# Output projections of two attention layers begun on the finished heads, during the last head's attention

## The chip, the core and the metric

The kernel runs on one core of a Trainium2 chip. Its engines work beside each other, each through its own list of instructions in order: TensorE (PE), VectorE (DVE), ScalarE (ACT), GpSimd (POOL) and SyncE (SP, which issues loads). They meet at semaphores. The metric is the device time of one execution in microseconds, the median of the runs; less is better.

## The reference

A network of six mixing and two feed-forward layers in float32, for 512 tokens of width 1024. The change touches the ends of the first two layers. Both have the same form: heads of attention, each times a gate, side by side as `y` (512 x 1024), then `y @ w_out`, a norm and the residual sum.

```python
# layer 0, dilated: 16 heads of 64, three groups of keys per head, joined by their log-denominators
y = o.reshape(B, S, DIL_WIDTH).astype(h.dtype) * jax.nn.silu(gate)
return y @ w_out
# layer 1, differential: 8 heads of 128
a = p[:, 0] - lam * p[:, 1]
o = rmsnorm(o, subln) * (1.0 - lambda_init)
y = o.reshape(B, S, DIFF_WIDTH) * jax.nn.silu(gate)
return y @ w_out
# around each layer
h = h + rmsnorm(y, norm_post[i])
```

## The kernel before

**Products.** Each float32 matrix is split in two parts of a narrower type: the high part (`uh`, `wh`) is a copy by ACT, the low part (`ul`, `wl`) the difference, which DVE makes for the input and POOL for the weights. A product is three matmuls (`three`, L418): high with high, low with high, high with low.

**Weights.** They stream in tiles of 128 x 1024. SP loads a tile into one of two slots of `raw` (L328) in two halves, once POOL has done the half that was there; ACT writes `wh` (`split`, L979), once the tile four back is used up (`tile_used`); POOL writes `wl` (L389) and signals `lo_ready`. From the first output projection on, `wh` and `wl` are rings of four slots.

**The dilated layer** works in stages of ten input tiles. A stage projects one pair of heads and computes the attention of the pair before it, a piece behind each tile: scores (L485), maxima on DVE (L1624), exponentials on ACT (L1099), weights on DVE (L1727), transposes on PE (L581), copies to `H` on ACT (L1146), and behind the last block PV (L593 to L606) and the gated result into `F` on DVE (L1714). `dil_last` computes the last pair, 7, with no tile beside it. "Head 7" below means this pair, and k counts the pairs: k is also the row block of `w_out` that goes with it. **The differential layer** has four tiles in a stage and the same scheme (transposes L492, values L497); its output is normed on DVE (L1776 to L1788), turned by PE (L678) and gated (L1796). The last stage is `diff_stage(None, 7, 0)`.

**Barriers.** `bound()` drains PE, ACT and DVE and lets none go on before the three have come to it. One stands ahead of each of the two projections.

**The output projection** has its tokens in the rows: 4 token blocks (t) by 2 column halves of 512, 8 k of 128 each. The first column half uses tiles b to b+3 (`tok_block`): tile j for the four blocks, two k each, banks 0 to 3. The second half uses b+4 to b+7 (`last_tokens`), block 0 with all four tiles first, then block 1, then 2 and 3 by turns, banks 4 to 7, beside the norms of the blocks that are done. ACT copies F to `uh` (`split_input`, L1031), DVE makes `ul` (`split_lo`, L1584): k = 0 and 1 ahead of the barrier, k = 2 to 7 behind it. PSUM has eight banks; scores use 2 and 3 (the dilated last head also 0 and 1), transposes 4 and 5, outputs 6, V's transposes 7. The next layer's first tiles start by token halves (`first_tiles`) in the banks that the projection used first.

The order of the work is the order in which each engine's function is written. ACT also issues DMAs: the gains (`ask_gain`) and, behind PV of the last dilated head, the input x into `H`, which held the weights until then (L1190).

## Time and profile before

| | |
|---|---|
| median of 3 runs | 2588.49 us (2584.99 to 2589.3) |
| profiled execution | 2583.04 us, span 2581.2 us |
| PE busy | 2409.3 us, 93% |
| DVE, ACT, POOL busy | 1184.4, 1102.8, 1036.0 us |
| mean granted clock of TensorE | 0.968 of full |

Times within the execution count from the start of the span. The profile's rows give the start, the busy time, the line and what is written and read; the number in square brackets is how long the engine idled before it, and who ended that.

### The profile page before, as it was taken

To read this page: it belongs to the slowest core of one execution; us is meant where nothing else is said; L and a number is where in the kernel's file an instruction comes from. 1 tells how busy PE (TensorE), PEld (TensorE's weight loads), DVE (VectorE), ACT (ScalarE), POOL (GpSimd) and SP (SyncE) were. 2 spreads that over 40 slices of the span, in tenths; PEclk is the share of its full clock that TensorE was granted. 3 is DMA by queue.
4 is the path that set the end of the run, shared out by engine and by line. 5 is a ranking of instruction groups with operands and counts; after the bars stand their busy time and mean duration, and the time that the engine had idled before them with its cause. 6 is when DMAs were issued, how large, how long until landed. Compare 5 with 4: busy or idle time off the path is not lost.

```text
span 2581.2 us, 40224 instructions
## 1 busy us (share of the span) xinstructions
PE 2409.3 (93%) x13062; PEld 1959.2 (76%) x13062; DVE 1184.4 (46%) x2431; ACT 1102.8 (43%) x2396; POOL 1036.0 (40%) x750
## 2 busy tenths in 40 slices
PE   7999999997999969997999999999888999999998
PEld 6777777776877748775878888888755878888887
DVE  4455554552667754266443432222776324522224
ACT  4433333334544435454554533232565544533322
POOL 4444343433433303451471354444411652444442
PEclk9999999997999969998999999999998999999999
DMA  5333333323322212220341233232212331232322
GB/s 189 103 96 94 93 99 91 94 82 103 94 82 79 74 35 74 83 89 25 101 145 50 82 107 98 91 100 94 88 52 66 115 123 50 94 98 94 98 89 82
DMA packets 126067, 232.02 MB, mean 90 GB/s; under 512 B 17120, under 2 KB 17248, under 8 KB 125920
## 3 DMA queue, kind: packets, MB, share of 16 engines
q1 hardware_dynamic: 123072, 219.56, 27.5%
q10 hardware_dynamic: 2848, 10.49, 1.1%
q8 instruction: 95, 1.56, 0.3%
q14 instruction: 52, 0.43, 0.1%
HBM read 208.48 MB, written 2.10 MB: 82 GB/s over the span
## 4 chain that ended last, share of the span: by engine, by line
PE 45%; issue 29%; POOL 10%; DVE 6%; DVEq 4%; ACT 3%; ACTq 1%; DMA 1%; POOLq 0%; SPq 0%
PE PS L418 39%; POOL wl L389 10%; DVEq L1500 3%; PE PS L485 2%; DVE work L1661 1%; PE PS L497 1%; DVE work L1657 1%; ACTq L1100 1%; DVE work L1624 1%; ACT work L1099 1%; DVEq L1625 1%; PE PS L606 1%; PE PS L630 1%; PE PS L581 0%; DVE work L1727 0%
## 5 line engine op out<-in xcount | busy, mean ns | idle before, releaser
L389 POOL TENSOR_TENSOR wl<-raw,wh 128x512 fp32r<-128x512 f32 x746 | 1035.7, 1411 | 1517.6 <-ACT wh L979 1516.3
L418 PE MATMUL PS<-uh,wh 128*128 128x512 f32 (+1 forms) x2120 | 801.0, 378 | 21.8 <-DVE ul L1550 8.5
L418 PE MATMUL PS<-uh,wl 128*128 128x512 f32 (+1 forms) x2120 | 785.9, 371 | 0.0
L418 PE MATMUL PS<-ul,wh 128*128 128x512 f32 (+1 forms) x2120 | 784.6, 370 | 0.0
L979 ACT ACTIVATE wh<-raw 128x512 fp32r<-128x512 f32 x746 | 430.1, 623 | 373.5 <-PE PS L418 319.5
L418 PEld LDWEIGHTS PS<-uh,wh 128*128 128x128 f32 x2120 | 404.9, 191 | 104.7 <-issue 17.7
L418 PEld LDWEIGHTS PS<-uh,wl 128*128 128x128 f32 x2120 | 403.6, 190 | 68.3
L418 PEld LDWEIGHTS PS<-ul,wh 128*128 128x128 f32 x2120 | 404.7, 191 | 64.0 <-issue 1.0
L418 PE MATMUL PS<-wh,hid_sb 128*128 128x512 f32 x1024 | 322.1, 396 | 0.0
L1118 ACT ACTIVATE work<-PS 128x512 f32<-128x512 f32 (+1 forms) x156 | 89.8, 575 | 404.6 <-PE PS L418 331.8
L418 PEld LDWEIGHTS PS<-wh,hid_sb 128*128 128x128 f32 x1024 | 192.4, 188 | 46.1
L418 PE MATMUL PS<-wl,hid_sb 128*128 128x512 f32 x512 | 202.5, 395 | 0.0
L418 PE MATMUL PS<-wh,uh 128*128 128x512 f32 x448 | 177.6, 396 | 8.6 <-DVEq L1495 6.5
L418 PE MATMUL PS<-wh,ul 128*128 128x512 f32 x448 | 176.5, 394 | 0.0
L418 PE MATMUL PS<-wl,uh 128*128 128x512 f32 x448 | 176.3, 394 | 0.0
L485 PE MATMUL PS<-work 64*32 64x128 f32 (+8 forms) x1568 | 144.8, 363 | 20.5 <-DVEq L1949 7.6
L2073 DVE TENSOR_TENSOR work<-work,PS 128x512 f32<-128x512 f32 x96 | 66.0, 688 | 178.1 <-PE PS L418 178.1
L2055 DVE TENSOR_TENSOR work<-work 128x512 f32<-128x512 f32 x64 | 47.6, 743 | 214.4 <-ACT work L1404 214.4
L1099 ACT ACTIVATE work<-work,stat 128x512 f32<-128x512 f32 (+3 forms) x160 | 97.3, 609 | 109.8 <-DVEq L1625 109.7
L485 PEld LDWEIGHTS PS<-work 64*32 64x32 f32 (+2 forms) x1568 | 73.5, 145 | 60.5 <-issue 34.6
L418 PEld LDWEIGHTS PS<-wl,hid_sb 128*128 128x128 f32 x512 | 96.3, 188 | 23.2
L497 PE MATMUL PS<-work 128*128 128x128 f32 (+1 forms) x720 | 97.8, 298 | 15.6 <-ACT work L1105 15.6
(226 smaller groups left out, 2401.9 us busy)
## 6 DMA issues: line engine op xcount, KB each, us to landing
raw<-tiles_dram SPq DMA_DIRECT2D x746, 256.0 KB, 2.7
work<-work SPq DMA_DIRECT2D x296, 64.0 KB, 2.0
gB<-post_dram ACTq DMA_DIRECT2D x8, 512.0 KB, 3.7
H<-x_dram SPq DMA_DIRECT2D x4, 512.0 KB, 6.2
H<-x_dram ACTq DMA_DIRECT2D x4, 512.0 KB, 4.9
work<-mem_dram ACTq DMA_DIRECT2D x2, 1024.0 KB, 5.0
out_dram<-H ACTq DMA_DIRECT2D x4, 512.0 KB, 2.6
cst<-consts_dram SPq DMA_DIRECT2D x1, 644.0 KB, 5.0
```

The source lines that it names most:

```text
L389: nc.gpsimd.tensor_tensor(w_of(wl, slot)[:, hc], raw[:, s, hc], w_of(wh, slot)[:, hc].bitcast(F32), ALU.subtract).then_inc(lo_ready, 1)
L418: last = nc.tensor.matmul(out, a, b, start=start and m == 0, stop=stop and m == 2)
L485: ins = nc.tensor.matmul(o, q, k, start=first, stop=last)
L497: last = nc.tensor.matmul(out, a, b, start=n == 0, stop=n == len(pairs) - 1)
L606: last = nc.tensor.matmul(out, dv(ap, g)[:, r, h64], dpt[:, :, h, at:at + 32], start=False, stop=g == 2 and r == 3)
L630: last = nc.tensor.transpose(PS[:, XB, t * P:(t + 1) * P], src, ident)
L979: nc.scalar.activation(w_of(wh, slot)[:, hc], raw[:, raw_slot, hc], ACT.Copy).then_inc(hi_ready, 1)
L1099: last = nc.scalar.activation(sm, sm, ACT.Exp, bias=bias, scale=-1.0, accum_out=d)
L1118: nc.scalar.activation(dst, PS[:, bank, 0:width], ACT.Copy).then_inc(lin_evac, 1)
L1500: v.drain()
L2055: v.tensor_tensor(hs(j), hs(j), hs(j), ALU.mult)
L2073: v.tensor_tensor(ys, ys, PS[:, bk, :], ALU.add).then_inc(y_evac, 1)
```

## The change

PE computes 28 of the 32 groups (t, k) of the first column half, k = 0 to 6, between the pieces of the last head's attention (`begin`), in the order `EARLY`: k = 0 to 5 for blocks 0 to 2, then block 3, then k = 6 for all; k = 7 follows as soon as the last head is in `F`. The accumulators move to banks 0, 1, 7 and 2, the second half's to 3, 4, 5 and 6 (`MOVED`), and the next layer's first tiles likewise; block 3 comes late since bank 2 holds scores. The dilated last head's scores use banks 2 and 3 alone. ACT and DVE split k = 0 to 6 between their parts of the attention, ACT also the weight tiles b to b+3. The barriers ahead of the two projections are gone. The diff is cut to the parts that the steps speak of; the rest passes `banks` on.

```diff
@@ -301,8 +301,13 @@
         BIG = 3e38
-        def half_ps(half, k):
-            return PS[:, 4 * half + 2 * (k // 4) + k % 2, k % 4 // 2 * 256:k % 4 // 2 * 256 + 256]
+        PLAIN, MOVED = [0, 1, 2, 3, 4, 5, 6, 7], [0, 1, 7, 2, 3, 4, 5, 6]
+
+        def half_ps(half, k, banks=PLAIN):
+            return PS[:, banks[4 * half + 2 * (k // 4) + k % 2], k % 4 // 2 * 256:k % 4 // 2 * 256 + 256]
+
+        EARLY = [(t, k) for k in range(6) for t in range(3)] + [(3, k) for k in range(6)]
+        EARLY += [(t, k) for k in (6, 7) for t in range(4)]
...
@@ -537,24 +542,42 @@
-            def out_projection(name):
-                u0 = 8 * (c.add("u") - 1)
+            def begin(n, u0, first, last):
+
+                for t, k in EARLY[first:last]:
+                    slot, ts, ws = slot_of(n + k // 2), slice(t * P, (t + 1) * P), slice(k % 2 * 512, k % 2 * 512 + 512)
+                    if t == 0:
+                        pe.wait_ge(lo_ready, 2 * n + k + 1)
+                        pe.wait_ge(u_ready, u0 + k + 1)
+                    ins = three(PS[:, MOVED[t], :], w_of(wh, slot)[:, ws], w_of(wl, slot)[:, ws], uh[:, k, ts],
+                                ul[:, k, ts], k == 0, k == KT - 1, w_is_lhs=False)
+                    if t == 3 and k % 2 == 1:
+                        ins.then_inc(tile_used, 1)
+                    elif k == KT - 1:
+                        ins.then_inc(bank_done, 1)
+
+            def out_projection(name, begun=None):
                 c.add("out", 8)
                 n = BASE[name]
-                tok_block(n, slot_of(n), KT, [t for t in range(TT)], u0=u0)
+                if begun is None:
+                    banks = PLAIN
+                    tok_block(n, slot_of(n), KT, [t for t in range(TT)], u0=8 * (c.add("u") - 1))
+                else:
+                    banks = MOVED
+                    begin(n, begun, 28, 32)
                 n += 4
                         k, ws = 2 * j + kk, slice(kk * 512, kk * 512 + 512)
-                        last = three(PS[:, 4 + t, :], w_of(wh, slot)[:, ws], w_of(wl, slot)[:, ws], uh[:, k, ts],
+                        last = three(PS[:, banks[4 + t], :], w_of(wh, slot)[:, ws], w_of(wl, slot)[:, ws], uh[:, k, ts],
                                      ul[:, k, ts], k == 0, k == KT - 1, w_is_lhs=False)
                     pe.wait_ge(y_copied, c.get("out") - 4)
-                    return half_transposes(0)
+                    return half_transposes(0, banks)
                 return last_tokens(n, piece, turn_rows)
...
@@ -632,14 +655,24 @@
-                ap = 1 - par
+                ap, n, u0 = 1 - par, BASE["dil_out"], 8 * (c.add("u") - 1)
                 pe.wait_ge(aux_taken, A * 9 + 6)
                 dil_scores(A, ap, 0)
-                for n in range(TT):
-                    if n < 3:
-                        dil_scores(A, ap, n + 1, (SB0, SB1) if n % 2 else (0, 1), ahead=2 if n else 1)
-                    dil_transposes(A, n)
+                dil_scores(A, ap, 1)
+                begin(n, u0, 0, 6)
+                dil_transposes(A, 0)
+                dil_scores(A, ap, 2)
+                begin(n, u0, 6, 12)
+                dil_transposes(A, 1)
+                dil_scores(A, ap, 3)
+                begin(n, u0, 12, 15)
+                dil_transposes(A, 2)
+                begin(n, u0, 15, 18)
+                dil_transposes(A, 3)
+                begin(n, u0, 18, 24)
                 dil_pv(A, ap)
+                begin(n, u0, 24, 28)
+                return u0
...
@@ -651,10 +684,7 @@
                 dil_stage(i * 2 + 3, i * 2 + 2, 1)
-            dil_last(7, 0)
-            bound()
-            if on("dil_out"):
-                u_diff = out_projection("dil_out")
+            u_diff = out_projection("dil_out", dil_last(7, 0))
...
@@ -709,6 +739,8 @@
                         diff_values(*unit)
+                    if u0 is not None and j < 3:
+                        begin(BASE["diff_out"], u0, (0, 6, 9)[j], (6, 9, 12)[j])
                     if before and j == 3:
...
@@ -720,13 +752,16 @@
                 diff_stage(7, 6, 1)
-                diff_stage(None, 7, 0)
+                u_out = 8 * (c.add("u") - 1)
+                diff_stage(None, 7, 0, u_out)
+                begin(BASE["diff_out"], u_out, 12, 18)
                 diff_transposes(7, 1, 3)
                 diff_values(7, 1, 3)
+                begin(BASE["diff_out"], u_out, 18, 24)
                 diff_outputs(7)
-                bound()
+                begin(BASE["diff_out"], u_out, 24, 28)
             if on("diff_out"):
-                u_ev = out_projection("diff_out")
+                u_ev = out_projection("diff_out", u_out)
...
@@ -1166,12 +1202,24 @@
+                b = BASE["dil_out"]
+                split_g(b)
+                act.wait_ge(y_taken, 7)
+                split_input(0, 3)
                 dil_exps(A, 0)
-                for n in range(TT):
-                    if n < 3:
-                        dil_exps(A, n + 1)
-                        split_g(80 + n)
-                    dil_pt(A, n)
+                split_g(b + 1)
+                split_input(3, 5)
+                dil_exps(A, 1)
+                dil_pt(A, 0)
+                split_g(b + 2)
+                split_input(5, 6)
+                dil_exps(A, 2)
+                dil_pt(A, 1)
+                split_input(6, 7)
+                split_g(b + 3)
+                dil_exps(A, 3)
+                dil_pt(A, 2)
+                dil_pt(A, 3)
...
@@ -1182,15 +1230,12 @@
             dil_last(7)
-            if on("dil_out"):
-                split_first(y_taken, 2)
-                ask_gain("dil")
-                act.wait_ge(pv_done, 32)
-                for t in range(TT):
-                    act.dma_start(H[:, t, :], x[t * P:(t + 1) * P, :]).then_inc(x_in[t], 16)
-            bound()
-            if on("dil_out"):
-                out_projection("dil_out", ("norm_pre", 8))
+            ask_gain("dil")
+            act.wait_ge(pv_done, 32)
+            for t in range(TT):
+                act.dma_start(H[:, t, :], x[t * P:(t + 1) * P, :]).then_inc(x_in[t], 16)
+            act.wait_ge(y_taken, 8)
+            out_projection("dil_out", ("norm_pre", 8), begun=True)
...
@@ -1224,6 +1270,16 @@
                             gate_tile(n, fgraw, fgexp, bank, L + 8)
+                    if last and j < 3:
+                        if j == 0:
+                            act.wait_ge(tile_used, BASE["diff_out"])
+                            act.wait_ge(head_done, 5)
+                        split_input((0, 2, 4)[j], (2, 4, 5)[j])
+                        if j == 1:
+                            split_g(BASE["diff_out"] + 3)
+                    if last and j == 3:
+                        act.wait_ge(head_done, 6)
+                        split_input(5, 6)
                     if before and j == 0:
...
@@ -1250,14 +1306,13 @@
                 diff_pt(7, 3)
-                if on("diff_out"):
-                    split_first(head_done, 2)
                 diff_squares(7, 1)
-                if on("diff_out"):
-                    ask_gain("diff")
-                bound()
+                act.wait_ge(head_done, 7)
+                split_input(6, 7)
+                ask_gain("diff")
+                act.wait_ge(head_done, 8)
             if on("diff_out"):
-                out_projection("diff_out", ("g_mix_pre", 0))
+                out_projection("diff_out", ("g_mix_pre", 0), begun=True)
...
@@ -1594,9 +1649,11 @@
-            def out_projection(gain, mem_of=None, again=False):
-
-                split_lo(2, KT)
+            def out_projection(gain, mem_of=None, again=False, begun=False):
+
+                banks = MOVED if begun else PLAIN
+                if not begun:
+                    split_lo(2, KT)
                 if mem_of is not None:
...
@@ -1745,12 +1803,19 @@
                 dil_consume(A, 8, ap)
+                dil_max(A, 0)
+                split_lo(0, 2)
                 silu(dgate(ap), dgate(ap), dgexp, A * 10 + 10)
-                dil_max(A, 0)
-                for n in range(TT):
-                    if n < 3:
-                        dil_max(A, n + 1, (SB0, SB1) if n % 2 else (0, 1))
-                    dil_weights(A, n)
+                dil_max(A, 1)
+                dil_weights(A, 0)
+                split_lo(2, 4)
+                dil_max(A, 2)
+                dil_weights(A, 1)
+                split_lo(4, 6)
+                dil_max(A, 3)
+                dil_weights(A, 2)
+                split_lo(6, 7)
+                dil_weights(A, 3)
...
@@ -1761,12 +1826,10 @@
             dil_last(7, 0)
-            if on("dil_out"):
-                split_lo(0, 2)
             dil_result(7, 1)
-            bound()
-            if on("dil_out"):
-                out_projection(("norm_pre", 8), again=True)
+            v.drain()
+            split_lo(7, KT)
+            out_projection(("norm_pre", 8), again=True, begun=True)
...
@@ -1831,12 +1895,16 @@
                         diff_weights(A - 1, par, 3)
+                    if last:
+                        split_lo(0, 2)
                     silu(fgate(ap), fgraw, fgexp, A * 4 + (LIN["diff"] + 4))
                         diff_weights(A, ap, j - 1)
+                    if last:
+                        split_lo((2, 4, 5)[j - 1], (4, 5, 6)[j - 1])
                     if L is not None and j != 2:
...
@@ -1854,13 +1922,12 @@
                 diff_weights(7, 1, 3)
-                if on("diff_out"):
-                    split_lo(0, 2)
                 diff_norm(7, 1)
+                split_lo(6, 7)
                 diff_result(7, 1)
-                bound()
+                split_lo(7, KT)
             if on("diff_out"):
-                out_projection(("g_mix_pre", 0))
+                out_projection(("g_mix_pre", 0), begun=True)
```

On PE, in the last dilated head: scores of block 1, transposes of block 0 and scores of block 2 of before.

```order
L485 MATMUL PS<-work 128x256 [waits max_ready]
L485 MATMUL PS<-work 128x256
L485 MATMUL PS<-work 32x64 x16
L581 MATMUL PS<-cst,work 128x128 [waits probs_ready,pt_ready]
L581 MATMUL PS<-cst,work 128x128 x7
L485 MATMUL PS<-work 128x256 [waits max_ready]
L485 MATMUL PS<-work 128x256
L485 MATMUL PS<-work 32x96 x16
L581 MATMUL PS<-cst,work 128x128 [waits probs_ready,pt_ready]
L581 MATMUL PS<-cst,work 128x128 x7
L485 MATMUL PS<-work 128x256 [waits max_ready]
```

The same place after the change, from the last of six groups (L423 is `three`, L604 the transposes, L490 the scores).

```order
L423 MATMUL PS<-wh,uh 128x512
L423 MATMUL PS<-wh,ul 128x512
L423 MATMUL PS<-wl,uh 128x512
L604 MATMUL PS<-cst,work 128x128 [waits probs_ready,pt_ready]
L604 MATMUL PS<-cst,work 128x128 x7
L490 MATMUL PS<-work 128x256 [waits max_ready]
L490 MATMUL PS<-work 128x256
L490 MATMUL PS<-work 32x96 x16
L423 MATMUL PS<-wh,uh 128x512 [waits u_ready,lo_ready]
L423 MATMUL PS<-wh,ul 128x512
L423 MATMUL PS<-wl,uh 128x512
```

Six groups, 18 matmuls, now stand between the scores of block 1 and the transposes of block 0, and the next six behind the scores of block 2.

On ACT, around the DMAs behind PV of the same head, before: uh<-F are k = 0, 1 and 2 to 7, wh<-raw is tile b+3.

```order
L1146 ACTIVATE H<-PS 128x1024 [waits pv_done,pt_psum] x2
L1031 ACTIVATE uh<-F 128x512 [waits y_taken]
L1031 ACTIVATE uh<-F 128x512
L1094 DMA gB<-post_dram 128x1024
L1190 DMA H<-x_dram 128x1024 [waits pv_done]
L1190 DMA H<-x_dram 128x1024 x3
L1031 ACTIVATE uh<-F 128x512 [waits phase_end]
L1031 ACTIVATE uh<-F 128x512 x5
L979 ACTIVATE wh<-raw 128x512 [waits half_tile_loaded_1_0,tile_used]
L979 ACTIVATE wh<-raw 128x512 [waits half_tile_loaded_1_1]
```

After it: uh<-F is k = 7, wh<-raw are tiles b+4 and b+5 (L1182 is L1146 of before, L1066 L1031, L1014 L979).

```order
L1182 ACTIVATE H<-PS 128x1024 [waits pv_done,pt_psum] x2
L1130 DMA gB<-post_dram 128x1024
L1236 DMA H<-x_dram 128x1024 [waits pv_done]
L1236 DMA H<-x_dram 128x1024 x3
L1066 ACTIVATE uh<-F 128x512 [waits y_taken]
L1014 ACTIVATE wh<-raw 128x512 [waits half_tile_loaded_0_0,tile_used]
L1014 ACTIVATE wh<-raw 128x512 [waits half_tile_loaded_0_1]
L1014 ACTIVATE wh<-raw 128x512 [waits half_tile_loaded_1_0,tile_used]
L1014 ACTIVATE wh<-raw 128x512 [waits half_tile_loaded_1_1]
```

Of k = 0 to 7 only k = 7 is left behind the DMAs, without a barrier, and tile b+4 comes directly after it.

On DVE, the end of the differential layer before: the norm's product, the gated result, six low parts.

```order
L1785 TENSOR_TENSOR stat<-stat 128x4
L1788 TENSOR_SCALAR work<-PS,stat 128x128 x4
L1796 SCALAR_TENSOR_TENSOR F<-PS,stat,work 128x512 [waits head_tr]
L1584 TENSOR_TENSOR ul<-F,uh 128x512 [waits uh_ready,phase_end]
L1584 TENSOR_TENSOR ul<-F,uh 128x512 [waits uh_ready] x5
L1608 TENSOR_TENSOR work<-PS,gB 128x512 [waits y_squared,gain_in]
L1608 TENSOR_TENSOR work<-PS,gB 128x512 [waits y_squared] x4
```

After it (L1639 is L1584 of before, L1859 L1796).

```order
L1851 TENSOR_SCALAR work<-PS,stat 128x128 x4
L1639 TENSOR_TENSOR ul<-F,uh 128x512 [waits uh_ready]
L1859 SCALAR_TENSOR_TENSOR F<-PS,stat,work 128x512 [waits head_tr]
L1639 TENSOR_TENSOR ul<-F,uh 128x512 [waits uh_ready]
L1665 TENSOR_TENSOR work<-PS,gB 128x512 [waits y_squared,gain_in]
L1665 TENSOR_TENSOR work<-PS,gB 128x512 [waits y_squared] x4
```

k = 6 went ahead of the last result, k = 7 stays behind it, and the others went into the last stage.

## Rows read from the trace of the kernel before

**Rows 1.** The page: the span, TensorE's busy time, the loads of weight tiles.

```profile
span 2581.2 us, 40224 instructions
...
PE 2409.3 (93%) x13062; PEld 1959.2 (76%) x13062; DVE 1184.4 (46%) x2431; ACT 1102.8 (43%) x2396; POOL 1036.0 (40%) x750
...
raw<-tiles_dram SPq DMA_DIRECT2D x746, 256.0 KB, 2.7
```

**Rows 2.** The windows view, five stretches; its first line names the columns.

```profile
core 0: us, PE busy (x) PEld busy (x) DVE busy (x) ACT busy (x) POOL busy (x), PEclk, DMA share, GB/s
581.70:617.27 35.57, 20.18 (x242) 15.54 (x240) 13.14 (x33) 15.65 (x30) 7.68 (x6) 0.66 0.23 65
617.27:640.96 23.69, 23.69 (x97) 19.44 (x98) 3.70 (x6) 7.74 (x14) 10.59 (x8) 0.93 0.49 168
588.00:600.00 12.00, 7.65 (x80) 5.32 (x88) 3.49 (x12) 7.39 (x14) 5.01 (x4) 0.50 0.20 50
624.00:640.00 16.00, 16.00 (x72) 13.27 (x71) 0.00 (x0) 3.46 (x6) 7.72 (x7) 1.00 0.38 117
925.70:969.00 43.30, 18.59 (x67) 11.83 (x66) 22.30 (x89) 12.66 (x44) 0.00 (x0) 0.57 0.04 14
```

**Rows 3.** The timeline of PE: start, us, line, operation, count, idle before.

```profile
502.74 1.09 PE L593 MATMUL PS<-H,work 128*64 128x128 f32 x16
...
506.17 0.75 PE L630 MATMUL PS<-cst,work 128*128 128x128 f32 x4
...
518.27 0.87 PE L485 MATMUL PS<-work 64*128 64x128 f32 x36
...
551.42 1.04 PE L581 MATMUL PS<-cst,work 128*128 128x128 f32 x8
...
585.36 1.30 PE L485 MATMUL PS<-work 64*128 64x256 f32 x36 [2.22 <-DVEq L1625]
...
617.27 0.50 PE L418 MATMUL PS<-wh,uh 128*128 128x512 f32 x1 [2.07 <-ACTq L970]
```

**Rows 4.** The timeline of PE: starts of matmuls three apart, twice.

```profile
618.90 0.63 PE L418 MATMUL PS<-wl,uh 128*128 128x512 f32 x1
...
620.18 0.63 PE L418 MATMUL PS<-wl,uh 128*128 128x512 f32 x1
...
624.44 0.39 PE L418 MATMUL PS<-wh,uh 128*128 128x512 f32 x1
...
625.12 0.39 PE L418 MATMUL PS<-wh,uh 128*128 128x512 f32 x1
```

**Rows 5.** The timeline of ACT behind the last dilated head.

```profile
615.23 1.79 ACTq L1190 DMA_DIRECT2D H<-x_dram  x4
617.29 3.23 ACT L1031 ACTIVATE uh<-F 128x512 fp32r<-128x512 f32 x6 [7.49 <-ACTq L970]
```

**Rows 6.** The timeline of DVE at the same place.

```profile
618.03 3.70 DVE L1584 TENSOR_TENSOR ul<-F,uh 128x512 fp32r<-128x512 f32 x6 [1.74 <-ACT uh L1031]
```

**Rows 7.** The timeline of POOL: two tiles.

```profile
621.12 3.00 POOL L389 TENSOR_TENSOR wl<-raw,wh 128x512 fp32r<-128x512 f32 x2 [14.12 <-ACT wh L979]
...
630.79 2.53 POOL L389 TENSOR_TENSOR wl<-raw,wh 128x512 fp32r<-128x512 f32 x2 [2.91 <-ACT wh L979]
```

**Rows 8.** Waits in the differential tail (total, times, longest), then PE's timeline there.

```profile
PE PS L492 <- DVEq L1817: 16.1, 5, 5.8
...
934.35 0.45 PE L492 MATMUL PS<-cst,work 128*128 128x128 f32 x1 [0.78 <-DVEq L1817]
...
956.12 1.09 PE L492 MATMUL PS<-cst,work 128*128 128x128 f32 x4 [2.79 <-DVEq L1817]
...
966.93 1.12 PE L678 MATMUL PS<-cst,work 128*128 128x128 f32 x4 [6.96 <-DVEq L1790]
```

**Rows 9.** The timeline of ACT: the squares of head 7, the projection's last tile.

```profile
960.00 0.28 ACT L1237 ACTIVATE work<-PS 128x128 f32<-128x128 f32 x1 [1.13 <-PE PS L497]
...
992.98 1.15 ACT L979 ACTIVATE wh<-raw 128x512 fp32r<-128x512 f32 x2 [4.29 <-PE PS L418]
```

More of the change, by code:

```diff
@@ L1016, in norm_hi, with half_hi @@
                 c.add("u", KT)
-            def half_hi(gain, half):
+            def half_hi(gain, half, banks=PLAIN):
                 for k in range(KT):
@@ L1543, in norm_lo, with half_lo @@
                         .then_inc(u_ready, 1)
-            def half_lo(gain, half):
+            def half_lo(gain, half, banks=PLAIN):
                 for k in range(KT):
```

64 lines of the change are left out of this document (34 added, 30 removed).

## The prediction, made before the result was known

> **What bounds the kernel now.** I read the page's first lines, then the timeline of TensorE around the two places that the change touches, then the same stretches in the windows view, and last the other engines' timelines there. The page says that TensorE is the bound nearly everywhere: 2409.3 us busy in a span of 2581.2 [rows 1]. The reader is to see where it is not. When the last dilated head has no further input tile beside it, TensorE has only that head's attention: 20.18 us of work in 35.57 us, at a granted clock of 0.66 [rows 2]. Head 7 of the differential layer is the same: 18.59 of 43.30 us, at 0.57 [rows 2]. Behind each tail comes the first half of an output projection, 96 matmuls of 512 columns. It needs 23.69 us behind the dilated layer [rows 2], and from 969.01 to about 992.98 behind the other, since there ACT's next splitting of a tile is released by the last of them [rows 9]. A tail is bound by a chain that crosses PE, DVE and ACT for every block of queries; in the differential one PE waits five times for DVE's weights, 16.1 us in all [rows 8]. So the question is how many of the 2 x 96 matmuls fit into the holes, and what they push back.
>
> **The sum of the dilated tail.** Three matmuls make a group (one token block, one k). At the full clock a group takes 0.68 us (start to start 624.44 to 625.12), at the half clock 1.28 (618.90 to 620.18) [rows 4]. A projection half is 32 groups; 28 go ahead of the last head's end, 4 (k = 7) remain behind it.
> PE's work from 581.70, at full clock: V's transposes 0.6; four scores of 0.87 to about 1.6, 5.3; four sets of transposes at 1.04, 4.2; PV 3.43 (502.74 to 506.17) [rows 3]; 32 groups, 21.8. Sum 35.3 us. The old tail took 35.57 with none of them.
> Waits that stay on PE: 1.5 us before the second scores (2.2 before, but silu, some 0.7 us, now lies behind the first maximum), 0.7 for the weights of block 2, and 0.6 for k = 7, which needs PV, then 1.79 us of ACT's four DMA issues, 0.54 of ACT and 0.62 of DVE [rows 5, 6], against 2.7 us of k = 6 groups. Sum 2.8.
> Clock: before, it fell after such holes and came back only behind a full stretch. With groups in the holes PE hardly rests, so I charge one stretch of half clock, 1.7 us; the ends are 0 and the whole tail (a rival below).
> So the first half ends at 581.70 + 35.3 + 2.8 + 1.7 = 621.5, against 640.96 now (617.27 + 23.69). Gain 19.5 us. The removed barrier is in it: its price was the 2.07 us before 617.27, which is ACT's DMA issues [rows 3, 5]; their order does not change, only who waits for them does.
>
> **What is late next.** The tiles of the second half. Tile b+4 may be split only when tile b is used, and that is the first signal of token block 3, whose groups now stand just ahead of PV. ACT comes to it even later: behind PV, the DMA issues and k = 7, some 2.4 us after PV. Before, POOL's two subtractions of a tile, 2.53 us [rows 7], lay between uses 5.44 us apart. Now four tiles are wanted within 5.4 us. From PV's end: 2.4 + 0.55 (first half tile split) + 8 x 1.27 = 13.1, + 1.36 for the last piece, 14.5. Without that limit it would be 2.7 + 0.6 + 2.7 + 5.4 = 11.4. Stall about 3.2 us, in three holes, and I charge 1.5 us for the clock there (ends 0 and 3). The loads are just hidden: a half tile lands 2.7 us after its issue [rows 1] and POOL asks for it some 3.8 us after the slot came free; beside the 2 MB of H it may cost up to 2 more. Dilated gain: 19.5 - 3.2 - 1.5 = 14.8.
> In one row POOL's pair took 3.00 us (621.12) and not 2.53; DVE's subtractions from k = 2 on ran beside it from 618.03 to 621.73 [rows 6, 7]. The Trainium skill, page "GPSIMD Engine Reference", section "1. Specifications", says that GpSimd shares its SBUF interfaces with VectorE and is slowed by its instructions with two SBUF inputs. The trace agrees. The change speaks against itself here by that rule: the same subtractions of DVE now stand beside POOL's tiles of the first half. But those have slack, and beside the four that stall only k = 7's runs; by the rule the stall is 3.4, by the row alone 3.2.
>
> **The differential tail.** Behind PV of head 7 (ACT's squares start at 960.00) the squares and the norm last until PE's transposes at 966.93, and this stays [rows 8, 9]. Now the first half ends at 992.98, 33.0 us after 960.00. After: six groups of token block 3 lie under the norm (4.1 of 6.9 us); then DVE's low part of k = 6 (0.62) beside the transposes, 2.7 us of k = 6, during which the result, ACT's and DVE's parts of k = 7 are made (0.75 + 0.1 + 0.6 + 0.65), and 2.7 of k = 7: 6.9 + 0.7 + 5.4 = 13.0. Gain 20.0. The clock will be at half after the hole under the norm: minus 2.4 (ends 0 and 4.8, eight groups at 1.28).
> Ahead of PV, in PE's order: six groups between block 3's values of head 6 and block 0's transposes, where PE idled 0.8: +3.3 (half clock +6.9); three in a hole of 2.70 and three in one of 5.8: 0; six in one of 2.79 (956.12): +1.3 (half clock +4.9) [rows 8]. ACT: two high parts and a tile, 2.2 us, stand ahead of the squares and of block 0's probabilities: partly under the groups, +1. DVE: 0.6 ahead of the norm of head 6. Against it: the 18.59 us of PE work at 0.57 [rows 2] run partly at full clock, some 5 us on the chain (ends 0 and 8). Together +1 (ends -4 and +8). The same stall and clock: 3.2 + 1.5. Differential gain: 20.0 - 2.4 - 1.0 - 4.7 = 11.9.
>
> **Cost nothing:** the other PSUM banks (same count of columns), the first tiles of the next layer in banks 0, 1, 7, 2 (already copied when XB is written), single-buffered dilated scores (scores 3 wait for maximum 2, which ends during the groups), SP's queue (its loads wait for POOL as before). What follows the first half, ACT's squares and norms, shifts along with the pieces; ACT reaches the first of them about 0.6 us later against PE than now, under 5.4 us of the next piece.
>
> **Sum.** 14.8 + 11.9 = 26.7 us. The profiled execution took 2583.04 us for a span of 2581.2; it becomes 2556.3. The median of the runs, 2588.49, lies 5.4 above that execution; by the median it is 2561.8, and that is my forecast: 2562.
>
> **Rivals.**
> 1. Supply is no limit and the clock stays up: both stalls (6.4), their clock (3.0) and the clock terms of the tails (4.1) fall away: 2548. For it: clock 1.00 over 624 to 640 and wherever PE was full [rows 2]. Against it: POOL's 2.53 us per tile is firm.
> 2. The chain pays more. PE takes its instructions in order, so a group that is begun stands ahead of the transposes when the weights come, and ACT's and DVE's added parts (8 x 0.54, 8 x 0.62 per tail) stand ahead of exps and maxima. At the upper ends 14 us go: 7 more ahead of the differential PV, 2.4 of its clock, 3.9 for three dilated block periods each 1.3 longer, 1 for the loads: 2576. For it: in the differential tail DVE is busy 22.30 of 43.30 us on the chain [rows 2].
> 3. Slower. The clock never comes up in the tails. Dilated: 20.18 + 28 x 1.28 + 2.8 + 4 x 1.28 = 63.9 against 59.3 (35.57 + 23.69) now, +4.6; differential: 18.59 + 35.8 + 8 of waits + 5.1 = 67.5 against 67.3, and the second halves start at half clock, +2 each: about +9, 2597. It decides from the point where the half clock holds over nearly all of both tails. For it: 588 to 600 at 0.50 with PE busy 7.65 of 12 us [rows 2]. Against it: there PE had holes of 2 to 3 us each period, which the groups fill, and at 624 to 640, without holes, it was 1.00. The Trainium skill, page "TensorE: Matmul & The Clock Gate", section "HAM oscillation — how this bites in real kernels", says that bursts of matmuls with waits between them fall back to the low clock at each wait. The trace agrees for the old tail (0.66, 0.57) [rows 2].
> 4. The groups do not start early, because the parts of k = 0 or tile b come late, and only the barriers go: about 2586.
>
> **Chances.** Forecast 0.60 (its own range 2554 to 2570), rival 1 0.13, rival 2 0.19, rival 3 0.05, rival 4 0.03. The range 2548 to 2577 leaves out most of 3 and 4 and the far edges of 1 and 2. A measurement of this kernel tells 0.2% (5.2 us) from no change; so faster 0.92, the same 0.04, slower 0.04.
>
> **What would show it.** Right: PE's rows of three matmuls between scores and transposes, the last head's PV only some 5 us earlier or later than now, four groups behind the next wait, clock above 0.85 over the dilated tail; three holes of about 1 us on PE in the second half's first token block, released by POOL; POOL's eight subtractions back to back there. Wrong: PE waiting for DVE's low parts, a clock of 0.5 through the tails, PV of head 7 more than 8 us later than now, or holes that ACT or a load releases.

## The result and the profile after

The changed kernel takes 2564.75 us, median of four runs (2562.92 to 2569.45); the kernel before took 2586.74 in the same measurement. The ratio is 0.9924 (0.9912 to 0.9937), a gain of 22.0 us where the prediction's sum was 26.7. Measured again on another occasion it took 2562.57 against 2585.05, ratio 0.991 (0.9896 to 0.9923). The profiled execution took 2565.09 us.

The first lines of the profile after, which answer to [rows 1], and the windows view of three stretches (the columns are named in its first line), which answers to [rows 2]:

```profile
span 2563.3 us, 40218 instructions
...
PE 2402.4 (94%) x13062; PEld 1953.0 (76%) x13062; DVE 1186.8 (46%) x2431; ACT 1103.5 (43%) x2396; POOL 1036.2 (40%) x750
```

```profile
core 0: us, PE busy (x) PEld busy (x) DVE busy (x) ACT busy (x) POOL busy (x), PEclk, DMA share, GB/s
583.23:624.00 40.77, 35.95 (x337) 27.71 (x336) 20.61 (x39) 21.86 (x42) 13.57 (x11) 1.00 0.34 109
626.00:637.00 11.00, 7.50 (x20) 5.56 (x21) 2.77 (x4) 7.31 (x17) 5.01 (x5) 0.69 0.47 153
913.95:961.05 47.10, 32.58 (x139) 24.04 (x139) 24.89 (x94) 16.72 (x50) 3.09 (x2) 0.82 0.07 23
```

The matmuls are the same 13062. The dilated tail now holds its own attention and the whole first half of the projection: 583.23 to 624.0, 40.8 us, where tail and first half took 59.3. Its granted clock is 1.00 (2.4 GHz) where it was 0.66. The differential tail went from 0.57 to 0.82 only, and between 626 and 637 there is a stretch of 0.69 that was 1.00 before.

The timeline of PE in the dilated part (start, us, line, operation, count, and in brackets the idle time before it and what ended it). First the kernel before, two landmarks for each part: the last head's first scores, and a row of the next layer that no edit touches. Then the kernel after.

```profile
582.26 0.88 PE L485 MATMUL PS<-work 64*128 64x128 f32 x36
...
691.56 0.60 PE L708 MATMUL PS<-cst,work 128*128 128x128 f32 x4
...
930.74 0.80 PE L485 MATMUL PS<-work 64*128 64x128 f32 x4
...
1031.38 0.39 PE L418 MATMUL PS<-uh,wh 128*128 128x256 f32 x1 [1.46 <-DVE ul L1550]
```

```profile
583.79 0.88 PE L490 MATMUL PS<-work 64*128 64x128 f32 x36
...
593.05 1.07 PE L604 MATMUL PS<-cst,work 128*128 128x128 f32 x8 [1.26 <-DVEq L1786]
...
606.35 1.07 PE L604 MATMUL PS<-cst,work 128*128 128x128 f32 x8 [1.63 <-DVEq L1786]
...
614.42 1.09 PE L616 MATMUL PS<-H,work 128*64 128x128 f32 x16
...
621.30 0.47 PE L423 MATMUL PS<-wh,uh 128*128 128x512 f32 x1 [0.42 <-DVE ul L1639]
...
626.09 0.50 PE L423 MATMUL PS<-wh,uh 128*128 128x512 f32 x1 [0.45 <-POOL wl L394]
...
631.15 0.79 PE L423 MATMUL PS<-wh,uh 128*128 128x512 f32 x1 [3.40 <-POOL wl L394]
631.74 0.63 PE L423 MATMUL PS<-wh,ul 128*128 128x512 f32 x1
632.17 0.63 PE L423 MATMUL PS<-wl,uh 128*128 128x512 f32 x1
...
681.29 0.60 PE L738 MATMUL PS<-cst,work 128*128 128x128 f32 x4
```

From landmark to landmark it was 109.30 us (582.26 to 691.56) and is 97.50 (583.79 to 681.29): the dilated part gives 11.8. PV starts at 614.42, 30.6 us after the first scores (before, 26.7 us after them, at 608.91). Behind it stand three waits: 0.42 for DVE's low part of k = 7, then 0.45 and 3.40 for tiles of POOL. Behind the wait of 3.40 the matmuls start 0.43 us apart, not 0.23: the low clock (1.2 GHz). The other engines there, ACT first, then POOL:

```profile
617.96 1.79 ACTq L1236 DMA_DIRECT2D H<-x_dram  x4
...
620.33 2.18 ACT L1014 ACTIVATE wh<-raw 128x512 fp32r<-128x512 f32 x4
627.90 1.23 ACT L1014 ACTIVATE wh<-raw 128x512 fp32r<-128x512 f32 x2 [5.39 <-DMA raw<-tiles_dram]
```

```profile
621.03 5.01 POOL L394 TENSOR_TENSOR wl<-raw,wh 128x512 fp32r<-128x512 f32 x4 [15.53 <-ACT wh L1014]
628.61 4.98 POOL L394 TENSOR_TENSOR wl<-raw,wh 128x512 fp32r<-128x512 f32 x4 [2.57 <-ACT wh L1014]
```

and the transfers of 614 to 632 (KB of one, median us from issue to landing):

```profile
H<-x_dram ACTq DMA_DIRECT2D x4, 512.0 KB, 5.2
raw<-tiles_dram SPq DMA_DIRECT2D x6, 256.0 KB, 4.0
```

POOL does two tiles, rests 2.57 us, and does two more. It rests because ACT rests 5.39 us for a load: the loads of b+6 and b+7 run beside the 2 MB of H.

The differential part, PE and ACT:

```profile
919.01 0.80 PE L490 MATMUL PS<-work 64*128 64x128 f32 x4
...
926.67 0.27 PE L497 MATMUL PS<-cst,work 128*128 128x128 f32 x1
...
940.80 0.87 PE L497 MATMUL PS<-cst,work 128*128 128x128 f32 x3 [5.83 <-DVEq L1880]
...
950.78 0.60 PE L497 MATMUL PS<-cst,work 128*128 128x128 f32 x4
...
960.18 0.66 PE L708 MATMUL PS<-cst,work 128*128 128x128 f32 x4 [2.84 <-DVEq L1853]
961.05 0.68 PE L423 MATMUL PS<-wh,uh 128*128 128x512 f32 x1 [0.22 <-DVE ul L1639]
...
973.87 0.50 PE L423 MATMUL PS<-wh,uh 128*128 128x512 f32 x1 [1.40 <-POOL wl L394]
...
991.17 1.09 PE L459 MATMUL PS<-cst,work 128*128 128x128 f32 x8 [1.15 <-DVE work L1586]
...
1009.74 0.39 PE L423 MATMUL PS<-uh,wh 128*128 128x256 f32 x1 [1.45 <-DVE ul L1605]
```

```profile
953.26 0.28 ACT L1293 ACTIVATE work<-PS 128x128 f32<-128x128 f32 x1 [1.25 <-PE PS L502]
...
971.84 0.63 ACT L1014 ACTIVATE wh<-raw 128x512 fp32r<-128x512 f32 x1 [1.35 <-DMA raw<-tiles_dram]
972.38 0.58 ACT L1111 ACTIVATE work<-PS 128x512 f32<-128x512 f32 x1
```

Landmarks: 100.64 us before (930.74 to 1031.38), 90.73 after (919.01 to 1009.74), a gain of 9.9. With the dilated 11.8 that is 21.7, and the medians say 22.0. The head's squares start 34.25 us after its first scores (953.26); before it was 29.26 [rows 9].

### The profile page after: what moved, and what is told of

Read it like the earlier page. It is cut to its first block, busy times and chain, and to the rows that moved or that the text cites. A ratio compares the mean times of both kernels' runs of the same rounds, so it can differ in the third digit from the quotient of the medians.

```text
span 2563.3 us, 40218 instructions
## 1 busy us (share of the span) xinstructions
PE 2402.4 (94%) x13062; PEld 1953.0 (76%) x13062; DVE 1186.8 (46%) x2431; ACT 1103.5 (43%) x2396; POOL 1036.2 (40%) x750
## 4 chain that ended last, share of the span: by engine, by line
issue 54%; PE 22%; POOL 21%; ACT 1%; DVE 1%; POOLq 1%; DMA 0%; ACTq 0%; DVEq 0%; SPq 0%
POOL wl L394 21%; PE PS L423 20%; PE PS L490 1%; PE PS L502 0%; DMA raw<-tiles_dram 0%; POOLq L393 0%; DVE H L1649 0%; POOLq L402 0%; PE PS L459 0%; ACT work L1111 0%; ACT work L1043 0%; ACT wh L1014 0%; PE PS L497 0%; DVE work L1586 0%; DVE work L1665 0%
## 5 line engine op out<-in xcount | busy, mean ns | idle before, releaser
L423 PE MATMUL PS<-uh,wh 128*128 128x512 f32 (+1 forms) x2120 | 801.0, 378 | 21.8 <-DVE ul L1605 8.5
L423 PE MATMUL PS<-ul,wh 128*128 128x512 f32 (+1 forms) x2120 | 784.7, 370 | 0.0
L423 PE MATMUL PS<-uh,wl 128*128 128x512 f32 (+1 forms) x2120 | 784.5, 370 | 0.0
L1014 ACT ACTIVATE wh<-raw 128x512 fp32r<-128x512 f32 x746 | 430.6, 623 | 351.1 <-PE PS L423 286.6
L423 PEld LDWEIGHTS PS<-uh,wh 128*128 128x128 f32 x2120 | 404.4, 191 | 104.6 <-issue 19.0
L423 PEld LDWEIGHTS PS<-uh,wl 128*128 128x128 f32 x2120 | 404.2, 191 | 68.3
L423 PEld LDWEIGHTS PS<-ul,wh 128*128 128x128 f32 x2120 | 405.0, 191 | 63.2 <-issue 0.7
L423 PE MATMUL PS<-wh,hid_sb 128*128 128x512 f32 x1024 | 322.0, 396 | 0.0
L423 PEld LDWEIGHTS PS<-wh,hid_sb 128*128 128x128 f32 x1024 | 192.4, 188 | 46.1
L423 PE MATMUL PS<-wl,hid_sb 128*128 128x512 f32 x512 | 202.5, 395 | 0.0
L423 PE MATMUL PS<-wh,uh 128*128 128x512 f32 x448 | 180.0, 402 | 11.0 <-POOL wl L394 5.2
L423 PE MATMUL PS<-wh,ul 128*128 128x512 f32 x448 | 176.8, 395 | 0.0
L423 PE MATMUL PS<-wl,uh 128*128 128x512 f32 x448 | 176.5, 394 | 0.0
L490 PE MATMUL PS<-work 64*32 64x128 f32 (+8 forms) x1568 | 144.2, 361 | 18.3 <-DVEq L2016 7.3
L490 PEld LDWEIGHTS PS<-work 64*32 64x32 f32 (+2 forms) x1568 | 73.5, 144 | 57.6 <-issue 33.3
L423 PEld LDWEIGHTS PS<-wl,hid_sb 128*128 128x128 f32 x512 | 96.3, 188 | 23.2
```

Of the source, the lines that this page charges most:

```text
L423: last = nc.tensor.matmul(out, a, b, start=start and m == 0, stop=stop and m == 2)
L490: ins = nc.tensor.matmul(o, q, k, start=first, stop=last)
L1014: nc.scalar.activation(w_of(wh, slot)[:, hc], raw[:, raw_slot, hc], ACT.Copy).then_inc(hi_ready, 1)
```

## The experiments

Each was compared with the kernel before on the same chip. "Dilated" and "differential" are the two stretches between the landmarks above.

| kernel | us | gain | ratio (interval) | dilated | differential |
|---|---|---|---|---|---|
| before | 2586.74 | | | 109.30 | 100.64 |
| after | 2564.75 | 22.0 | 0.9924 (0.9912-0.9937) | 97.50 | 90.73 |
| e0_after | 2562.57 | 22.5 | 0.991 (0.9896-0.9923) | 97.6 | 90.22 |
| e1_dil_only | 2576.22 | 11.0 | 0.9955 (0.9942-0.9967) | 97.2 | 100.87 |
| e2_diff_only | 2575.48 | 11.8 | 0.9958 (0.9945-0.9971) | 107.3 | 89.85 |
| e3_barriers | 2581.29 | 6.0 | 0.9979 (0.9969-0.9989) | 104.0 | 100.08 |
| e4_h_later | 2565.21 | 22.1 | 0.9914 (0.9899-0.9928) | 95.15 | 90.61 |
| e5_split_early | 2558.44 | 26.6 | 0.9894 (0.9878-0.991) | 91.33 | 91.30 |
| e6_spread | 2561.16 | 23.9 | 0.9899 (0.9884-0.9914) | 97.39 | 84.41 |
| e7_both | 2558.73 | 26.3 | 0.9886 (0.9866-0.9905) | 91.41 | 85.39 |
| e8_best | 2551.65 | 34.0 | 0.9871 (0.9854-0.9887) | 90.41 | 84.53 |
| e9_before_again | 2587.57 (one run) | | | 109.41 | 100.67 |
| e10_shift | 2585.64 | 0.0 | 1.0 (0.999-1.0009) | 111.06 | 100.37 |

**The two halves of the change, apart.** e1_dil_only keeps the dilated edits alone, e2_diff_only the differential ones alone; each leaves the other tail as before, with its barrier. The cut, in the dilated-only kernel:

```diff
-                diff_stage(None, 7, 0, u_out)
-                begin(BASE["diff_out"], u_out, 12, 18)
+                diff_stage(None, 7, 0)
                 diff_transposes(7, 1, 3)
                 diff_values(7, 1, 3)
-                begin(BASE["diff_out"], u_out, 18, 24)
                 diff_outputs(7)
-                begin(BASE["diff_out"], u_out, 24, 28)
+                bound()
```

> The dilated output projection begins early and its barrier goes; the differential one is as before, behind its barrier. My theory of the result (two tails, each with its own sum): the trace of the changed kernel moves the landmarks behind the dilated projection by 11.8 us against its own start and those behind the differential one by a further 9.9 us; so this kernel gains 11 to 13 us on the one before. Rival (the tails are not independent, or the gain comes from one of them): under 8 or over 17 us.

> The differential output projection begins early and its barrier goes; the dilated one is as before. My theory: 9 to 11 us gained on the kernel before, and with the dilated part alone the two add to the whole, 21 to 22 us. Rival: one of the two carries nearly all.

11.0 and 11.8 (a little above the 9 to 11 expected), together 22.8: the halves add up to the whole within their intervals, so neither needs the other. In each, the touched stretch is as short as in the full change. The untouched dilated stretch of e2 was 107.3 and not 109.3, its PV alone 1.5 us shorter because the clock came back sooner: a stretch that nobody edits can differ by that much between two traces.

**Only the barriers.** The kernel before with the two barriers out and only the waits left that the data need:

```diff
             dil_last(7, 0)
-            bound()
...
-            bound()
+            act.wait_ge(y_taken, 8)
...
                 diff_outputs(7)
-                bound()
...
-                bound()
+                act.wait_ge(head_done, 8)
```

> The kernel before with the two barriers taken out and nothing begun early (ACT waits for the last head's result in their place). My theory: what held PE in the dilated tail, 2.07 us, were ACT's four DMA issues ahead of the high parts of k = 2, and they stay ahead; PE can start k = 0 and 1 at once, behind PV, so up to 2 us are gained there and up to 1 us behind the differential layer: 0.5 to 3 us. Rival: the barriers were a large part of the gain, 5 us or more.

It gained 6.0, more than the 0.5 to 3 expected. The dilated stretch is 5.3 shorter; the differential one only 0.6. Of the 5.3, 1.5 lie ahead of the place where the barrier stood: PV ended earlier at a better clock, as it did in e2, whose dilated part is that of the kernel before, so the removal is not shown to be their cause. 2.07 are the wait before the projection [rows 3]. The rest, about 1.7, lies behind it: all of the projection's groups run at the full clock, where some took 1.28 us before [rows 4]. So the wait of 2.07 cost 3.8: its own length and the slow stretch behind it.

**What holds the tiles back.** e4_h_later issues the loads of H behind the splits of b+4 to b+6 instead of ahead of them:

```diff
-            act.wait_ge(pv_done, 32)
-            for t in range(TT):
-                act.dma_start(H[:, t, :], x[t * P:(t + 1) * P, :]).then_inc(x_in[t], 16)
             act.wait_ge(y_taken, 8)
...
                 for j in range(1 if begun else 0, 5):
+                    if late is not None and j == 4:
+                        late()
                     split_g(b + j + 3)
```

> The changed kernel with ACT's four loads of x into H issued behind the splitting of tiles b+4 to b+6, not ahead of k = 7. Theory of the load: the 3.40 us in which PE waits for tile b+6 of the dilated projection are its load landing 5.4 us after its issue beside the 2 MB of H, and the k = 7 parts come 1.8 us earlier, so the wait falls to 1 to 1.5 us, the clock stays up, and 3 to 6 us are gained on the changed kernel (25 to 28 on the one before). Theory of POOL, the term of my prediction: POOL's 2.5 us per tile sets it, the wait stays near 3 us and at most 2 us are gained.

PE's waits in e4, then ACT:

```profile
627.61 0.50 PE L423 MATMUL PS<-wh,uh 128*128 128x512 f32 x1 [0.94 <-POOL wl L394]
...
631.29 0.50 PE L423 MATMUL PS<-wh,uh 128*128 128x512 f32 x1 [2.04 <-POOL wl L394]
```

```profile
625.59 2.05 ACTq L1240 DMA_DIRECT2D H<-x_dram  x4
628.02 1.15 ACT L1014 ACTIVATE wh<-raw 128x512 fp32r<-128x512 f32 x2 [1.81 <-issue]
```

The 3.40 became 0.94 and 2.04, with no half clock behind them, and the dilated stretch is 2.35 shorter. With H out of the way the load of b+6 landed after 2.9 us, not 5.5, and POOL's first six subtractions run back to back; the last wait has another origin: ACT's four DMA issues (2.05 us) now stand ahead of the split of b+7. A new wait of 0.93 for DVE's normalised block, at 648.39, takes 1.1 us back. So the loads beside H were part of the stall, and not its root. By the medians e4 is like the changed kernel (22.1 against 22.0 and 22.5), where the first theory had asked for 3 to 6 us more. The second has its "at most 2 us", but not its wait that stays near 3.

**Split the tiles before PV is done.** e5_split_early makes ACT split b+4 and b+5 ahead of its wait for PV, in both layers:

```diff
             ask_gain("dil")
+            split_g(BASE["dil_out"] + 4)
+            split_g(BASE["dil_out"] + 5)
             act.wait_ge(pv_done, 32)
...
                 ask_gain("diff")
+                split_g(BASE["diff_out"] + 4)
+                split_g(BASE["diff_out"] + 5)
                 act.wait_ge(head_done, 8)
...
-                for j in range(1 if begun else 0, 5):
+                for j in range(3 if begun else 0, 5):
```

> The changed kernel with ACT splitting tiles b+4 and b+5 ahead of its wait for PV (dilated) or for the last result (differential), which their slots allow since block 3's groups stand ahead of that. Theory: the waits of PE for tiles in the second half (0.45 + 3.40 us and 1.40 us) come from ACT reaching these splits late; moved ahead, POOL and the loads of b+6 run under PV, all three waits go and with them the clock's half rate from 630.0 to 636.8: 6 to 9 us less than the changed kernel. Rival: PE then waits elsewhere, since tile b+7 is free only when k = 7 is done: under 3 us.

From PV to the end of the second half's first block one wait of PE is left, and of the second half's tiles POOL has done two by PV's end:

```profile
620.00 0.47 PE L423 MATMUL PS<-wh,uh 128*128 128x512 f32 x1 [0.63 <-DVE ul L1643]
```

```profile
610.99 4.99 POOL L394 TENSOR_TENSOR wl<-raw,wh 128x512 fp32r<-128x512 f32 x4 [7.00 <-ACT wh L1014]
```

All the supply waits are gone, and the half-clock stretch behind them: 6.2 us of the dilated stretch. The late splits in ACT's queue were the root. The median fell by 4.1 against the changed kernel in the same measurement (2562.57), and the slowest of e5's runs (2559.88) is below the fastest of the other's (2561.5); 6 to 9 were expected. The differential stretch got no shorter: it lost the supply wait and the wait of 991.17, and paid for that ahead of them. DVE, POOL and PE in e5 under head 7's norm:

```profile
949.34 0.16 DVE L1565 TENSOR_SCALAR stat<-stat 128x4 f32<-128x4 f32 x1
949.58 1.29 DVE L1567 TENSOR_SCALAR stat<-stat 128x4 int32<-128x4 int32 x1
950.94 1.14 DVE L1570 TENSOR_TENSOR stat<-stat 128x4 f32<-128x4 f32 x1
```

```profile
949.55 4.95 POOL L394 TENSOR_TENSOR wl<-raw,wh 128x512 fp32r<-128x512 f32 x4 [28.68 <-ACT wh L1014]
```

```profile
957.48 1.11 PE L708 MATMUL PS<-cst,work 128*128 128x128 f32 x4 [6.91 <-DVEq L1857]
```

DVE's norm consists of instructions of four columns. They take 0.16 to 0.18 us, but four of them took 1.14 to 1.29, one behind each of POOL's four subtractions, and PE's transposes waited 6.91 where they waited 2.84. In the changed kernel, without POOL beside them, all took 0.16 to 0.18. The Trainium skill, page "SBUF — State Buffer", section "SBUF: two separate sides", says that GpSimd and those instructions of VectorE that run in a two-port mode or have two SBUF inputs share a pair of ports under an exclusive lock, held for a whole instruction while the other blocks. The trace agrees: 1.14 to 1.29 beside POOL's 1.24 (4.95 for four). In which mode the one with a single tile as input (L1567) ran, the trace does not tell.

**The groups in other places.** e6_spread changes only where the differential groups stand: one, four and eight behind the first three blocks instead of six, three and three, and four ahead of the last transposes instead of six:

```diff
-                        begin(BASE["diff_out"], u0, (0, 6, 9)[j], (6, 9, 12)[j])
+                        begin(BASE["diff_out"], u0, (0, 1, 5)[j], (1, 5, 13)[j])
...
-                begin(BASE["diff_out"], u_out, 12, 18)
+                begin(BASE["diff_out"], u_out, 13, 17)
                 diff_transposes(7, 1, 3)
                 diff_values(7, 1, 3)
-                begin(BASE["diff_out"], u_out, 18, 24)
+                begin(BASE["diff_out"], u_out, 17, 24)
```

> The changed kernel with the differential tail's groups put in by the sizes of the holes: 1, 4, 8, 4 and 7 groups in place of 6, 3, 3, 6 and 6. Theory: the six ahead of head 7's first transposes moved these 4.1 us later and the six ahead of the last transposes another 2.5, PV came 5.0 us late, so 3 to 5 us are gained. Rival (DVE's and ACT's added parts, 8 x 0.62 and 8 x 0.54, hold the chain, or the clock falls in emptier holes): under 1.5 us.

```profile
919.58 0.80 PE L490 MATMUL PS<-work 64*128 64x128 f32 x4
...
923.49 0.41 PE L497 MATMUL PS<-cst,work 128*128 128x128 f32 x1
...
938.65 0.52 PE L497 MATMUL PS<-cst,work 128*128 128x128 f32 x3 [1.75 <-DVEq L1880]
...
954.31 0.66 PE L708 MATMUL PS<-cst,work 128*128 128x128 f32 x4 [2.17 <-DVEq L1853]
```

```profile
947.39 0.28 ACT L1293 ACTIVATE work<-PS 128x128 f32<-128x128 f32 x1 [1.25 <-PE PS L502]
```

Head 7's first transposes start 3.9 us after its first scores, not 7.7, and its squares 27.81 us after them, not 34.25: 6.4 earlier. The differential stretch is 6.3 shorter than the changed kernel's 90.73. The big wait before 940.80 (5.83) is now 1.75: the groups fill the hole that is there, instead of standing ahead of a transpose that is ready. In the medians 1.4 of it is seen (2561.16 against 2562.57, with runs that overlap), which is the rival's number and not its mechanism; where 3.2 of the rest went is below.

**Both, and the best.** e7_both is e5 and e6 together. e8_best keeps e6's places, splits early in the dilated layer alone (the differential early splits had cost DVE's norm), and issues H's loads behind ACT's part of k = 7:

```diff
+            split_g(BASE["dil_out"] + 4)
+            split_g(BASE["dil_out"] + 5)
             act.wait_ge(y_taken, 8)
...
+                if late is not None:
+                    late()
+                for j in range(3 if late is not None else 1 if begun else 0, 5):
                     split_g(b + j + 3)
```

> Both edits of the last two, tiles split early and groups spread. If they add: 9 to 13 us less than the changed kernel, 31 to 35 less than the one before. If the early splits fill the same time on ACT: no more than the better of the two.

> The best parts together: tiles b+4 and b+5 split ahead of PV in the dilated tail alone, the loads of x into H issued behind k = 7's high part there, and the differential tail's groups spread by the holes, with its tiles split as in the changed kernel. Theory: the early splits took 6.2 us out of the dilated stretch and the spread groups 6.1 out of the differential one, while early splits in the differential tail cost 1 us, since DVE's small instructions of the norm took 1.1 us each beside POOL's; so by the end of the differential projection this kernel is 33 to 35 us ahead of the one before, and 24 to 32 at the end, as later layers give some back. Rival (the two edits take the same time): no better than both together were, 26 us.

e7 by the landmarks is 6.1 and 5.3 shorter than the changed kernel, yet its median is that of e5: 26.3, and not the 31 to 35 of two edits that add. Its five runs lie far apart (2551.27 to 2561.59). e8 is 34.0 us under the kernel before, and 10.9 under the changed kernel's lower median (2562.57, from another measurement); no wait of PE stands between the dilated PV and the end of the second half's first block, and the supply waits of the differential part are 0.28 and 1.42. It beats both kernels. Against e7 its two stretches are only 1.0 and 0.9 shorter, while the medians are 7.1 apart; the two were measured on different occasions, and no run takes its choices one by one.

**The same kernels again, and a shift.** e0_after and e9_before_again are the two kernels unchanged. e10_shift is the kernel before with two more matmuls behind the first barrier, to move what follows in time:

```diff
             dil_last(7, 0)
             bound()
+            for _ in range(2):
+                nc.tensor.matmul(PS[:, XB, :], ident, cosT, start=True, stop=True)
```

> The changed kernel itself once more, beside the three below on one chip. By its first runs: 2564.75 against 2586.74, 22 us less, between 19 and 24.

> The kernel before once more, for its trace. In the untouched layers from 1020 to 1389 us every variant so far but one took 3 to 7 us longer than the one trace of before, with 43 to 55 us at the half clock in 1000 to 1400, where it had 37.5. Theory of the execution: this differs from run to run of one kernel, and this trace differs from the first by 2 us or more there. Theory of the program: the clock's state follows the program, this trace agrees with the first within 0.5 us.

> The kernel before with two more matmuls (fp32, 128x512, into a free bank, their results unused) behind the first barrier, which delays everything behind by 1.8 to 3.7 us. If the clock in the later layers depends on when they run, the delay at the end differs from the delay at the end of the dilated projection by 2 us or more; if not, it is the same within 1 us.

The spans of the two profiled executions gave only 17.9 us (2581.2 and 2563.3), while landmarks and medians say 22. Following the same instruction in both, the gain is 21.7 at 1013 us, 20.6 at 1268 and 17.5 at 1391, in layers that nobody edits. The kernel before, executed again, is 0.32 behind its first execution at 1268 and 4.52 at 1391: the theory of the execution holds. Windows view, 1268 to 1391, first execution, then the second:

```profile
1268.00:1391.00 123.00, 112.78 (x606) 97.69 (x606) 45.88 (x84) 61.81 (x127) 72.91 (x54) 0.97 0.38 116
```

```profile
1268.00:1391.00 123.00, 111.44 (x583) 95.91 (x582) 42.35 (x76) 60.28 (x121) 72.49 (x54) 0.95 0.36 116
```

606 and 583 matmuls in the same 123 us. The missing four microseconds are no more than two executions of the kernel before differ by: against the second one the profiled execution of after is 17.9 + 4.5 = 22.4 ahead at the end. Nine of the twelve other traces, the changed kernel's two among them, lose 2.5 to 4.2 us between 1300 and 1391 against the first trace of before; e4, e8 and e10 do not. That settles the 17.9.

It does not settle e6 and e7: they are 27.4 and 32.7 us ahead at 1013 and 24.2 and 29.5 at 1100, and e8 goes from 35.4 to 32.2 there (33.2 at the end). Behind a wait of PE of some 4.26 us for DVE that all have, these three have two half-clock stretches of 6.8 us each, where the changed kernel and the kernel before have two of 3.4. The three kernels with e6's places lose 3.2 us there and no other does, so it goes with that edit; how groups placed 100 us ahead bring it about, no run shows.

e10 decides nothing on its question. Its dilated stretch is 1.8 longer, as meant, but it was 3.1 us late before its edit began. Against the first trace of before its delay is 4.9 behind the dilated projection and 4.2 at the end, against the second 4.6 and -0.3.

## Why the prediction was right, and where its sizes were off

**The bound and the mechanism: right.** PE's holes in the two tails took the groups, the dilated clock went from 0.66 to 1.00 (above 0.85 was asked), and four groups stand behind the next wait. PV came 4.0 us later in the dilated tail ("some 5 us") and 5.0 later in the differential one (under 8). Rival 3 (clock never comes up) and rival 4 (only the barriers) are out: e3, which is rival 4, gained 6.0 of the 22.0.

**The total: gain 26.7 predicted, 22.0 measured.** The forecast of 2562 lies 2.8 us from the measured 2564.75, and that is nearer than the working earned: it was counted from a median of 2588.49, and the kernel before took 2586.74 in this measurement. The 4.7 us that are missing are 3.0 in the dilated part and 2.0 in the differential one.

**"Gain 19.5 us" for the dilated first half: right within 1.0.** It took 59.3 us from V's transposes and takes 40.8: 18.5. PE is busy 35.95 (35.3 in the sum). Of the 1.7 us charged for the clock nothing came; instead the waits were 4.8 (1.51 before the second scores, 1.26 and 1.63 before transposes, 0.42 for k = 7) where I had 2.8. That the total is so near is in part luck, since these two misses cancel.

The waits of 1.26 and 1.63 end with DVE's weights, and DVE was slowed there by POOL's tiles of the first half. Its two instructions took 1.93 us for block 2, beside POOL's pair of 602.95 to 605.49, and 0.88 for block 3, without POOL:

```profile
604.24 1.93 DVE L1785 TENSOR_SCALAR work<-work,stat 128x512 f32<-128x512 f32 x2
...
607.14 0.88 DVE L1785 TENSOR_SCALAR work<-work,stat 128x512 f32<-128x512 f32 x2
```

Likewise the low parts of k = 0 and 1 took 2.53 at 586.37 beside POOL, where the two of before took 1.29. I had asked only what DVE costs POOL there, which had slack; DVE had none. It is what e5 shows under the norm. No run takes it alone.

**"Stall about 3.2 us, in three holes": size 3.85, cause half wrong.** By my own terms it is 3.1 (14.5 - 11.4). I had POOL's 2.53 us per tile as the limit, all eight subtractions back to back, and wrote that holes which a load releases would be wrong. POOL paused 2.57 us for ACT, and ACT waited 5.39 for a load: b+6's, issued at 622.34 beside H, took 5.5 us, where the median of all 256 KB loads before was 2.7 [rows 1]. I had named that ("may cost up to 2 more") and priced it at nothing. The holes were two, 0.45 and 3.40, and not three of 1. e4 (loads apart: 2.35 back) and e5 (splits early: all back) show both parts.

**"1.5 us for the clock there": mis-sized.** One wait of 3.40 instead of three of 1 pulled the clock to half from about 630 to 637; 13 matmuls at 0.43 instead of 0.23 us make 2.6, with the start some 3. So 18.5 - 3.85 - 3 = 11.7, measured 11.8, predicted 14.8. This step holds half of the dilated miss of 3.0.

**"Together +1" ahead of the differential PV: mis-sized, +5.0.** I let the six groups ahead of block 0's transposes cost 3.3 and put 5 us of clock gain against it. Transposes 1 came 4.1 us later against the scores than before, those of the last block 6.4, and the gain at full clock stayed small, since each remaining hole (4.02, 5.83, 2.84) brought the half clock back: 0.82 and not 1.00. Rival 2 named this mechanism, at up to 7 more. e6 shows that it is the places of the groups: 6.4 back, with ACT's and DVE's added parts as they were.

**Behind PV: 13.0 + 2.4 predicted, 14.9 measured** (953.26 to 968.2). Right.

**"The same stall and clock: 3.2 + 1.5" in the differential layer: 1.40 by itself, 3.1 from the first half's end to the landmark (38.4 us before, 41.5 after).** No H load runs there, and the wait is 1.40. But ACT's splits, the last at 971.84, stand ahead of its squares of the first half, which start 4.2 us after that half's end (968.2 to 972.38), where they started 1.06 after it (992.98 to 994.04). The norms come late by that, and the next layer's transposes wait 1.15 at 991.17 for DVE's normalised block, a wait that did not exist. I had put this under **Cost nothing**, "0.6 us later": ACT was 3.1 later. e5 and e7, with early splits, do not have the wait; e6 and e8, with late ones, do (1.14 and 1.12). So the 4.7 of the sum were 3.1, made of a shorter stall and of a wait that the sum had at nothing. Sum: 20.0 + 0.5 (13.0 + 2.4 - 14.9) - 2.4 - 5.0 - 3.1 = 10.0, measured 9.9, predicted 11.9.

## What to carry to other kernels

When work is moved ahead into an engine's holes, look for the feeder queue next: here the tiles were split behind a wait for PV that they did not need, and two lines that split them ahead of it gave 6.2 us of one tail. Look also at what the feeder slows: in the other tail the same two lines put POOL beside DVE's norm, and nothing was gained there. Place the moved work behind the last ready step of the chain, sized to each hole that the trace shows; six groups ahead of the head's first transposes and six ahead of its last, in place of one and four, cost 6.4 us. Compare two kernels by landmarks around the edit before trusting a difference of whole spans: one execution was 4 us off in a layer that nobody touched.

## What the runs showed that was not expected

- Instructions of DVE on 128 x 4 elements took 1.14 to 1.29 us instead of 0.16, each behind one subtraction of POOL (1.24 us). Four of them under a norm moved PE's transposes by about 4 us.
- A wait of 2.07 us cost 3.8 in all: the half clock behind it cost 1.7 more. And a wait of 3.40 was followed by a stretch at half clock that cost some 3.
- A 256 KB load landed after 5.5 us beside four of 512 KB, and after 2.9 in e4, which issues the four later.
- The three kernels with e6's places, and no other, lost 3.2 us in a layer some 100 us further on, with two stretches of 6.8 us at the half clock instead of 3.4.
- Two executions of one kernel differed by 4.2 us between 1268 and 1391 us, at a granted clock of 0.97 and 0.95.
